# Expert slots split by token tile and gathered for two pairs at a time, with two divided places for expert weights

## The reference

```python
def hier_moe(xn, w_group, b_group, w_sub, b_sub, w1, w3, w2):
    ...
    gl = (t @ w_group).astype(jnp.float32) + b_group.astype(jnp.float32)
    gp = jax.nn.softmax(gl, axis=-1)
    g_w, g_sel = lax.top_k(gp, 1)
    ...
    sp = jax.nn.softmax(sl, axis=-1)
    top_p, top_e = lax.top_k(sp, MOE_TOPK)
    top_p = top_p / jnp.sum(top_p, axis=-1, keepdims=True)
    expert_id = g_sel * EXPERTS_PER_GROUP + top_e
    combine = jnp.einsum('tk,tke->te', g_w * top_p, jax.nn.one_hot(expert_id, N_EXPERTS, dtype=jnp.float32))
    out = jnp.zeros((b * s, d), jnp.float32)
    for e in range(N_EXPERTS):
        hid = jax.nn.silu(t @ w1[e]) * (t @ w3[e])
        out = out + combine[:, e:e + 1] * (hid @ w2[e]).astype(jnp.float32)
```

## Time and profile before

| what | value |
|---|---|
| median of 3 runs | 1027.51 us (1027.3 to 1027.52) |
| the profiled execution | 1027.36 us |
| its span | 1025.4 us |
| TensorE busy | 1000.4 us, 98% |
| VectorE, ScalarE, GpSimd busy | 512.3, 354.5, 86.1 us |
| experts' first product begins | 815.4 us |
| DMA | 227.57 MB, mean 222 GB/s; 396 to 421 GB/s in nearly all of the expert stage |

### The profile page before, as it was taken

The page is one execution under the profiler, slowest core; times in us unless marked ns, Lnnn a source line. Parts: engine busy times, 40 slices in busy tenths (PEclk is TensorE's granted clock), DMA queues, the critical chain, the costliest instruction groups (busy, mean ns, idle before and its releaser), DMA issues.

```text
span 1025.4 us, 15336 instructions
## 1 busy us (share of the span) xinstructions
PE 1000.4 (98%) x5676; PEld 711.1 (69%) x5676; DVE 512.3 (50%) x1398; ACT 354.5 (35%) x861; POOL 86.1 (8%) x140
## 2 busy tenths in 40 slices
PE   6999999999999999999999999999999999999996
PEld 2458554556887777988999877899999744444442
DVE  5559836447265667566865824953534510000004
ACT  5224133435043247245475124842121411111113
POOL 0061000032200004300000000000000010000000
PEclk9999999999999999999999999999999999999999
DMA  9972124762233421364354352058647799999996
GB/s 364 420 299 97 42 82 176 289 275 82 83 123 129 159 82 67 138 231 141 112 204 161 128 199 83 2 189 329 238 190 307 287 396 421 420 421 421 421 419 248
DMA packets 33942, 227.57 MB, mean 222 GB/s; under 512 B 4577, under 2 KB 4849, under 8 KB 8112
## 3 DMA queue, kind: packets, MB, share of 16 engines
q1 hardware_dynamic: 30784, 214.97, 53.3%
q10 hardware_dynamic: 1920, 9.80, 2.6%
q0 software_dynamic: 1168, 1.85, 0.5%
HBM read 222.15 MB, written 8.41 MB: 225 GB/s over the span
## 4 chain that ended last, share of the span: by engine, by line
PE 91%; DVE 6%; ACT 1%; issue 1%; DMA 1%; DVEq 0%; SPq 0%; ACTq 0%
PE lin L669 12%; PE sc L686 11%; PE lin L1398 11%; PE sc L792 6%; PE aux L1398 5%; PE lin L686 4%; PE aux L1246 4%; PE sc L892 4%; PE lin L856 3%; PE sc L1363 3%; PE sc L669 3%; PE aux L922 3%; PE sc L1071 3%; PE lin L908 3%; DVE UN L2281 2%; PE lin L938 2%
## 5 line engine op out<-in xcount | busy, mean ns | idle before, releaser
L669 PE MATMUL lin<-H,ring 128*128 128x256 f32 (+1 forms) x560 | 125.8, 385 | 0.0
L669 PEld LDWEIGHTS lin<-H,ring 128*128 128x128 f32 x560 | 106.0, 190 | 18.0 <-issue 4.2
L792 PE MATMUL sc<-H,ring 128*128 128x512 f32 (+1 forms) x192 | 67.3, 496 | 0.0
L1611 ACT ACTIVATE SP<-lin 128x512 f32<-128x512 f32 (+2 forms) x88 | 42.1, 486 | 71.9 <-PE lin L908 71.9
L2281 DVE SCALAR_TENSOR_TENSOR UN<-UN,cols 128x512 f32<-128x512 f32 (+1 forms) x120 | 66.7, 627 | 0.0
L2193 DVE CUSTOM_DVE_ANT_0 SP<-sc,CW,SK 128x512 f32<-128x512 f32 (+1 forms) x48 | 31.7, 661 | 53.6 <-PE sc L892 53.6
L1622 ACT ACTIVATE SP<-SP,ST 128x513 f32<-128x513 f32 (+4 forms) x88 | 53.9, 612 | 6.7 <-DVE ST L2196 6.4
L792 PEld LDWEIGHTS sc<-H,ring 128*128 128x128 f32 x192 | 34.8, 189 | 30.3 <-issue 25.6
L2848 DVE TENSOR_TENSOR PR<-lin,PR 128x512 f32<-128x512 f32 x8 | 5.5, 692 | 94.5 <-PE lin L1398 94.5
L892 PE MATMUL sc<-PR 64*128 64x256 f32 (+3 forms) x240 | 42.2, 434 | 2.9 <-DVE ST L2193 2.1
L1246 PE MATMUL aux<-Y,ring 128*128 128x256 f32 x192 | 42.0, 379 | 0.2 <-DVE PR L2642 0.2
(11 more groups left out here) (503 smaller groups left out, 1867.6 us busy)
## 6 DMA issues: line engine op xcount, KB each, us to landing
ring<-w_stream SPq DMA_DIRECT2D x119, 1024.0 KB, 6.7
SP<-w_stream SPq DMA_DIRECT2D x14, 1024.0 KB, 20.6
UN<-w_stream SPq DMA_DIRECT2D x10, 1024.0 KB, 19.5
PR<-w_stream SPq DMA_DIRECT2D x8, 1024.0 KB, 17.3
CW<-w_stream SPq DMA_DIRECT2D x8, 1024.0 KB, 17.8
X<-w_stream SPq DMA_DIRECT2D x8, 1024.0 KB, 17.1
Y<-w_stream SPq DMA_DIRECT2D x8, 1024.0 KB, 18.6
PR<-ada_in SPq DMA_DIRECT2D x5, 1024.0 KB, 26.2
```

Source lines behind the costliest of these rows:

```text
L669: m = mm(dst, w[:, k, :], rhs(k), start=n == 0, stop=n == KT - 1)
L792: m = mm(bank[:, 0:ns * SEQ], filling["w"][:, k, :], H[:, 0:ns, k, :], start=k == 0, stop=k == KT - 1)
L1611: fn(PT[:, g % TURNED, a:b], take()[:, 0:b - a], ACT.Copy).then_inc(lin_taken, 1)
```

## The change

1. **Slots by token tile.** Each expert's 64 slots are now 32 for tile 0 and 32 for tile 1 (`HALF`). Ranks are counted within a tile, so one placing product goes; the counts are kept per tile; another round of pairs is needed if an expert gets more than 32 tokens of one tile. A gather product of one tile then has 128 columns for 4 experts, that is, two pairs. No product adds up two tiles.
2. **Gathers for two pairs.** `gather_both` does pairs 2 and 3 during pairs 0 and 1, and pairs 4 and 5 during pairs 2 and 3, in four quarters: two in an even pair, one on either side of the transposes in an odd one. `COUPLED = 3` couples are handled so; pairs 6 and 7 are gathered one at a time (`gather`). Pair 4 gathers the first half of pair 6, pair 5 the second, pair 6 both halves of pair 7. ScalarE's copies and VectorE's selections follow; their loops over pairs are written out for the first six.
3. **Two divided places.** Place 20 is now half of `NB` and `SQ`, place 22 the piece of `E1` (PR) and the other half of `NB`. Unit 22 is fetched between ring units, amid the second block's last attention output product, and no longer behind unit 20.
4. **A gate product** moves from step 4 to step 3.
5. `SW`, the weighted selection of the last pair, is set to zero first.

```diff
-GATE_STEPS = (1, 4, 7, 10, 13, 16, 40, 42)
+GATE_STEPS = (1, 3, 7, 10, 13, 16, 40, 42)
...
+HALF = CAP // TT
...
+COUPLED = 3
...
-        SPLIT = (SQ.rearrange("p b n -> p (b n)"), E1[:, 3584:4608])
+        SPLIT = {20: (NB[:, 1024:2048], SQ.rearrange("p b n -> p (b n)")), SPLIT_PLACE: (E1[:, 3584:4608], NB[:, 0:1024])}
...
-            mm(bank[:, 16:32], before, MK1[:, 1, :], start=True, stop=False)
-            mm(bank[:, 16:32], one, MK1[:, 0, :], start=False, stop=True).then_inc(aux_ready, 1)
+            mm(bank[:, 16:32], before, MK1[:, 1, :], start=True, stop=True).then_inc(aux_ready, 1)
...
+            def gather_both(quarters):
+
+                for q in quarters:
+                    for a in (2 * q, 2 * q + 1):
                         for tt in range(TT):
+                            m = mm(both_pairs[:, a, :, tt, :], TK[:, tt, a * P:(a + 1) * P], SEL[:, tt, :], start=True, stop=True,
+                                   skip_group_check=True)
                     m.then_inc(e_gathered, 1)
...
-            gather()
+            gather_both(range(4))
...
-                else:
-                    pe.wait_ge(e_sel, i + 2)
-                    gather([0])
+                elif not isinstance(i, int):
+                    pe.wait_ge(e_sel, i - 1)
+                    gather(0)
+                elif i == 2 * COUPLED - 1:
+                    gather(1)
+                elif i % 2:
+                    gather_both([2])
                 pe.wait_ge(e_hidden, i + 1)
...
-                else:
-                    gather([1])
+                elif not isinstance(i, int):
+                    gather(1)
+                elif i % 2 == 0:
+                    pe.wait_ge(e_te_in, 2 * i + 4)
+                    pe.wait_ge(e_sel, i // 2 + 2)
+                    if i == 2 * COUPLED - 2:
+                        gather(0)
+                    else:
+                        gather_both([0, 1])
+                elif i < 2 * COUPLED - 1:
+                    gather_both([3])
                 pe.wait_ge(e_hid_in, i + 1)
...
             for n in range(RING_AT, RING_AT + SLOTS):
+                if n == RING_AT + 2:
+                    load_expert(BASE + SPLIT_PLACE, SPLIT_PLACE, (0,))
+                    sp.wait_ge(quarter_made, M_PART + m_at(1, 7))
+                    load_expert(BASE + SPLIT_PLACE, SPLIT_PLACE, (1,))
...
-            load_expert(BASE + SPLIT_PLACE, SPLIT_PLACE)
...
-                for x in range(2):
-                    ins = v.tensor_scalar(SEL[:, tt, x * CAP:(x + 1) * CAP], t0("iota"), 1.0, RF["place"][:, tt, x:x + 1], ALU.add, ALU.is_equal)
+                for x in range(4):
+                    ins = v.tensor_scalar(SEL[:, tt, x * HALF:(x + 1) * HALF], t0("iota")[:, 0:HALF], 1.0, RF["place"][:, tt, x:x + 1],
+                                          ALU.add, ALU.is_equal)
```

More of the change, by code:

```diff
@@ L183, in constants @@
     e = np.arange(N_EXP)
-    c0[:, slice(*C0["first_slot"])] = np.tile(TABLE * (CAP * (e % 2) - 1) + e // 2, TT)
+    c0[:, slice(*C0["first_slot"])] = np.concatenate([TABLE * (CAP * (e % 2) + HALF * t - 1) + e // 2 for t in range(TT)])
     c0[:, slice(*C0["couple"])] = np.tile(e // 2, TT)
@@ L1951, in _, with gathered @@
             last_pair = act.value_load(NP[0:1, 1:2], min_val=PAIRS - 1, max_val=PAIRS * PASSES - 1)
-            def gathered(n, halves=(0, 1)):
-                for half in halves:
-                    act.wait_ge(e_gathered, 2 * n + half + 1)
-                    fn(TE[:, 4 * half:4 * half + 4, :].rearrange("p k n -> p (k n)"), sc[:, 0, half * 512:(half + 1) * 512],
-                       ACT.Copy).then_inc(e_te_in, 1)
-            gathered(0)
+            both_pairs = sc.rearrange("p b (a q n) -> p (b a) q n", q=2, n=P)
+            one_pair = sc.rearrange("p b (a n) -> p (b a) n", n=P)
+            def gathered(n, half, landed):
+                act.wait_ge(e_gathered, landed)
+                a = slice(4 * half, 4 * half + 4)
+                src = both_pairs[:, a, n % 2, :] if isinstance(n, int) and n < 2 * COUPLED else one_pair[:, a, :]
+                fn(TE[:, a, :], src, ACT.Copy).then_inc(e_te_in, 1)
+            for half in range(2):
+                gathered(0, half, 2 * half + 2)
             def experts(i, last=False):
@@ L1964, in experts @@
                 if not last:
-                    gathered(i + 1, [0])
+                    act.wait_ge(e_third, i + 1)
+                    if not isinstance(i, int):
+                        gathered(i + 1, 0, 2 * i + 3)
+                    elif i % 2 == 0:
+                        for half in range(2):
+                            gathered(i + 1, half, 2 * i + 4)
+                    else:
+                        gathered(i + 1, 0, 2 * i + (3 if i == 2 * COUPLED - 1 else 4))
                 act.wait_ge(e_turned, i + 1)
@@ L1972, in experts @@
                 fn(YS[:, 0:512], aux[1][:, :], ACT.Copy).then_inc(e_y_lo, 1)
-            with act.Fori(0, last_pair) as i:
+            for i in range(2 * COUPLED):
+                experts(i)
+            with act.Fori(2 * COUPLED, last_pair) as i:
                 experts(i)
@@ L2841, in experts @@
                 if last:
-                    slots(SW, i, True, e_sw)
-                else:
+                    after(step(v.memset(SW[:, :, :], 0.0)))
+                    shares(i)
+                elif not isinstance(i, int):
                     dve.wait_ge(e_gathered, 2 * i + 2)
-                    slots(SEL, i + 1, False, e_sel)
+                    chosen(i + 1, 1)
+                elif i % 2 == 0:
+                    dve.wait_ge(e_gathered, 2 * i + 4)
+                    chosen(i + 2, 1 if i == 2 * COUPLED - 2 else 2)
                 dve.wait_ge(e_silu, i + 1)
@@ L2865, in experts @@
                     v.tensor_copy(YS[:, 512:1024], aux[0][:, :]).then_inc(e_y_hi, 1)
-            with dve.Fori(0, last_pair) as i:
+            for i in range(2 * COUPLED):
+                experts(i)
+            with dve.Fori(2 * COUPLED, last_pair) as i:
                 experts(i)
```

69 lines of the change are left out of this document (40 added, 29 removed).

## The result

| | before | after |
|---|---|---|
| median of 20 runs | 1027.47 us (1026.88 to 1028.22) | 1029.18 us (1028.58 to 1030.06) |
| ratio | | 1.0018, 95% interval 1.0012 to 1.0024 |
| span of the profiled execution | 1025.4 us | 1027.2 us |

The change makes the kernel slower by 1.7 us. The forecast was 1.3 us faster, 1026.2, with a range of 1023.4 to 1027.3.

The account below looks back on a forecast made before the run. The weight stream, with row read-back and VectorE's adds behind it, was taken to set the end. Stream 0.75 us earlier plus tail 0.55 made 1.3 us: 1027.51 - 1.3 = 1026.2 us, range 1023.4 to 1027.3.

Parts of the forecast that it names:

- What bounds the kernel: Expert stage: the path of weights, row read-back and VectorE's sums stands a few tenths behind the printed TensorE chain.
- The gathers: Expert pairs: sharing gathers saves TensorE about 7.5 us (5 to 11.3), nearly all then spent waiting for weights.
- The gate product: Before the third pair of scores: a 1.05 us TensorE wait goes, 0.45 us gained (0 to 1.05).
- The placing: Before the first gather: one 16-column product dropped, 0.22 us, with VectorE's eight selections in time; 0.2 us kept.
- The start of the stream: First weight fetch behind the 23 prefetched units, issued when unit 0 is used up: 0.65 us earlier.
- The divided places: Unit 22 fetched in halves amid the output product: counted as nothing, at most 0.5 us gained.
- The rule of the Trainium skill: Weight stream: about 2 us fixed cost per DMA; taken in series, three more divided fetches make it 6 us worse, near 1032.
- The stream's end: Last weight landing: moves only with the stream's start unless bytes are added; 0.75 us earlier (0.2 to 1.5).
- The tail: After VectorE's row sums: four last adds follow each other without waits, 0.55 us gained (0 to 0.6).
- Rival 1: Kernel's end: TensorE sets it, or unit 22 does shorten the stream; 3.4 to 4.0 us gained, 1023.8; 15%.
- rival 2: Expert stage: all of TensorE's saving arrives, 7.5 + 0.65 us, giving 1019.4; 3%.
- Rival 3: Weight stream: three more divided fetches lengthen it, at 2.3 us each ending 6.9 us later, 1033.1; 4%.

Follow-up runs that it names:

- experiment 6: Kernel before, with the row store's bound set to 0, so no expert row beyond row 0 is written: 1027.41 us, ratio 1.0.
- experiment 7: Kernel of experiment 1 with the gathers of pairs 0 and 2 done twice, 3.57 us more TensorE work: 1026.14 us, ratio 0.9988.
- experiment 1: Changed kernel with token tile 1's slots filled from the end (63, 62, ... of each 64): 1025.70 us, ratio 0.9983 against the kernel before.
- Experiment 4: Kernel before with only the changed kernel's two divided places, unit 22 fetched amid the last output product: 1027.42 us, ratio 1.0.
- experiment 2: Changed kernel with place 20 in one piece and unit 22 fetched where it was before: 1029.42 us, ratio 1.0019 against the kernel before.
- experiment 3: Kernel before with ranks 16 to 31 and 32 to 47 exchanging slots, slot list read by seven DMAs: 1030.09 us, ratio 1.0024.
- experiment 10: Changed kernel with tile 1's 32 slots turned by 16, slot list read by six DMAs: 1026.49 us, ratio 0.9992 against the kernel before.
- experiment 8: Kernel of experiment 1 with one of four row reads issued ahead of unit 95 and added early: 1025.19 us, ratio 0.9979.

## Why the prediction was wrong

**What bounds the kernel.** Right, and it decided the case: the stream of weights, the row read-back behind it and VectorE's sums behind that set the end of the changed kernel. TensorE's path and this one ended within a few tenths of each other before; experiment 6 shows that it was TensorE that came last, as the printed chain said.

**The gathers.** Right in kind: TensorE's saving of about 7.5 us turned into waits for weights, and experiment 7 gives it back nearly free. The size of the waits, 5.7 us where I had asked for 5 or more, is in part luck: the late stream makes some of them, and in experiment 1, where the stream is as short as before, they are 3.6. A little too high in size: over pairs 0 to 4 TensorE gained 6.0 us (pair 5 starts 6.9 us earlier, 0.9 of which was there at the start) where my terms make 6.6. In pair 1 the quarter gather of 0.89 did not quite cover VectorE's hidden product, which ended at 853.60 (0.70 from 852.90 in the chain above), so that pair gained 1.43 and not 1.8.

**The gate product.** Right: predicted 0.45 with the next wait at VectorE's second reader; measured 0.48 and exactly that wait, 0.41.

**The placing.** Predicted 0.2, measured some 0.05. The dropped product did give 0.22 us, but the first gather then waits about 0.1 more for VectorE's eight selections and takes 0.07 more itself (3.74 from its first pass to the first expert product on TensorE's time line, where it had 3.67).

**The start of the stream.** Predicted 0.65 earlier, measured 0.94. Of that, 0.24 lies before 604 us and is the difference between two executions, not the change; 0.48 is the gate product and 0.05 the placing. The other 0.17 arises between 613 and 808 us, and no run here says from what.

**The divided places.** I counted nothing and allowed 0.5 us. Experiment 4 gives nothing in the median (1027.42 with and without) and 0.4 in the stream's length, experiment 2 0.2 and 0.7. The rule of the Trainium skill weighed there, a fixed cost for each DMA (its section measures it on GpSimd's path; these fetches are SyncE's), taken in series, would have cost 6 us; the trace's reading stood.

**The stream's end: the step that failed.** The prediction said: "The end of the stream moves with this moment and with nothing else, unless bytes are added." No bytes were added, and it moved by 3.3 us the other way. The term of -0.75 was +2.3. The sentence took sixteen engines for one pipe of 421 GB/s. The runs fit sixteen queues of which the fullest ends the stream: 195.0 to 196.0 us where it carries 56 rows, 191.6 to 192.3 where it carries 33 to 40, 188.3 and 188.9 without rows. The change's first part, slots split by token tile, moves the used slots to other partitions, and GpSimd's row stores read from these partitions. I had priced that part for TensorE and VectorE only and did not ask which transfers touch the rows that it moves. The evidence of a price was in the trace of before: seven stores of rows in the middle of a full stream, which cost it 3.2 us, as experiment 6 shows.

**The tail.** Predicted -0.55, measured -0.5, with the four adds 2.48 us together, as worked out.

**The rivals.** Rival 1 (1023.8) and rival 2 (1019.4) did not come. Rival 3 had the sign, slower, but not the mechanism: its price per divided fetch is nil. The sign of being wrong that I had tied to it, a last landing later than 1009.3, did come (1011.6), but the halves are not its cause. The case that came true was not among the rivals. Put the layout right and the prediction's sum nearly holds: experiment 1 gives 1025.70 where it had 1026.2. Its row sums start 0.99 us earlier than before, where the sum had 0.75, and its tail is 0.5 shorter, where it had 0.55.

**The chances.** I gave 5% to slower by over 0.2%. The measured ratio is 1.0018, just inside "within 0.2%", but surely above 1. The range failed at its upper side, 1027.3, because it was made of the bounds of the terms that I had, and left nothing for a part of the change whose side effects I had not listed.

## What to carry to other kernels

When a change moves data to other partitions, list every DMA that reads or writes them, and count its rows on each DMA engine, not only in all; here it was an indirect store of which only the used rows carry bytes. Where a full stream sets the end, look at the DMA share in its last microseconds: here a share of 0.5 while transfers were outstanding was the sign of uneven load, and no mean over the stage (1.02, 420 GB/s) showed it. Laying the used rows out evenly took a few small instructions and gave 3.5 us.

## What the hardware showed that I had not expected

- Rows stored from two runs of partitions 32 apart hold up the weights more than the same rows from other partitions. Moving one run by 16 or mirroring it, with the same bytes, changed the length of the weight stream by 3.0 to 3.5 us in 192 (experiments 1, 3, 10), and moving them by 8 hardly at all (195.0 against 195.3). For the indirect row stores too, this agrees with the Trainium skill's formula ("DMA: Bandwidth & Descriptors", The descriptor swizzle); no view shows a single engine, so that it is the engines is worked out from the share of 0.52 and from how the layouts are ordered. No run separates the engine itself from anything else that the same partitions may share.
- A store of 0.26 MB, begun while the queue is full, lengthens the stream by 0.46 us (3.2 by 7) where its rows are spread and by 1.0 us (7.0 by 7) where they are crowded.
- With a queue 24 us deep the rate does not show the crowding while it happens: it stays at 420 GB/s, presumably because engines with fewer rows go on to later fetches. Single landings do show it (4.0 us apart for 2.5), and so does the end of the stream, where the share falls to 0.52.
- Two profiled executions of kernels that do the same up to that place reach the same scores at 613.03 and 613.96, 0.9 us apart (the changed kernel and experiment 8). A forecast of 0.45 us can be tested inside one stretch of the trace, not by its absolute time.
